# Stick-breaking with two heads of one feature tile a step and softplus in two rounded parts, and GLA products that alternate between the row halves

## The chip, the cores and the metric

The kernel runs on one core of one Trainium2 chip. The metric is the time of one execution on the device in microseconds, the median over several runs. Before the change it is 2219.93 us (three runs, 2217.63 to 2221.23).

## The reference

One layer of a decoder trunk over 1024 tokens of width 1024, in f32. Four causal token mixers work side by side on one wide projection `h @ w_in`: dilated window attention, a convolution module, gated linear attention (GLA) and stick-breaking attention. Each has its own output projection, is gated by a sigmoid of gate logits (also from `w_in`), and the sum goes through `w_out`; a squared-ReLU MLP follows. Two mixers matter here.

Stick-breaking, four heads of 64 features, for a query t and keys s < t:

```
z        = q.k / 8
log_keep = log_sigmoid(-z) where s < t, else 0
after    = sum of log_keep over the keys between s and t
w        = exp(log_sigmoid(z) + after) where s < t, else 0
o        = sum over s of w * v
```

Since log_sigmoid(-z) = -softplus(z) and log_sigmoid(z) = z - softplus(z), w is the exponential of z less a sum of softplus over the keys from s up to t.

GLA, four heads (64 key features, 128 value features), with a gate per token and key feature, in chunks (128 tokens in the kernel): inside a chunk a score of t and s is the sum over features of q k exp(cum_t - cum_s); across chunks a state (64 x 128 a head) is decayed and updated, and each chunk's output is values weighted by the scores plus the queries times the state.

## The kernel before

The stages follow each other in one program: front (adaLN, normalization, convolution), `stage_stick`, `stage_gla`, window attention, merge, tail. Each stage writes out every engine's queue by hand, in a block of its own, and the engines meet only at semaphores; an engine works its queue strictly in that order.

Through the mixers runs a second line of work, the dense projection by `w_in` (`class Dense`). A weight tile of 1024 x 128 is loaded (L125), ScalarE rounds it to fp32r as high part (L131), GpSimd subtracts to get the low part (L137), and `split_product` (L656) multiplies with three fp32r matmuls of 512 columns for each of eight feature tiles. Half of the tokens is one unit of 24 matmuls. In the mixers a unit is cut into three pieces of 9, 9 and 6 matmuls (`pieces`, L170), which TensorE's queue holds between the mixers' own products. `serve` (L183), `lower` (L192) and `move` (L200) do the same work for ScalarE, GpSimd and the DMA queue on SP.

**`stage_stick`** (from L2029). A step n is `STEPS[n] = (Q, r, a)`: a half Q of the queries (512), a key block a of 128 keys, counted downwards, and r, one half of the 128 rows of a feature tile. The two heads of a step are those in half r of the two feature tiles j. There are 24 steps: four segments (Q, r), of 4 and of 8 steps. In a block on the diagonal only the columns from the block on are worked on, so the widths are 128, 256, 384 and 512 columns a head, and the triangle in the block itself is cut by GpSimd (`keep_before`). The work of a step:

- `scores` (L2114): z for both heads, contraction over 64 rows, into `ps_z`.
- VectorE `take_scores` (L2182) scales it to `zs`. ScalarE `logs` (L2228, L2230, L2232): absolute value, Exp, Ln with 1 added. VectorE `softplus` (L2191): max(z, 0) plus that, into `sp_t`.
- `sums` (L2128): `ps_c` gets the product with the triangular matrix `reach`. VectorE `argument` (L2199): zs less `ps_c`. Then `pass_on` (L2138) adds the product with `below`, so that `ps_c` holds the whole block's sum for the next block.
- ScalarE `weights` (L2237) takes the exponential, `values` (L2150) adds w times v to `ps_o`, and `take` (L2204) copies a finished segment.

TensorE's loop is: scores(n), a piece, pass_on(n-2), sums(n-1), a piece, values(n-3). VectorE's is: argument(n-2), softplus(n-1), take_scores(n). ScalarE's is: logs(n), weights(n-2), its share of the dense work. GpSimd's is its dense work, the cut of the softplus of n, the cut of the weights of n-1.

**`stage_gla`** (from L1631) has four blocks. In the second one, the levels, a group is a pair of chunks: 8 matmuls of 128 columns over 64 rows (L1836), four of each row half, into a ring of three results; there are four groups in each of eight levels, and VectorE copies each under a mask (L1878) and prepares the next level's operands (L1866, L1867). A piece follows three of the four groups. The third block is the state loop over eight chunks: `update` (L1909), a piece in the first six, then for each head one product with the scores (L1926) and one with the state (L1929).

An f32 matmul in the source is two instructions in the trace, each with its own weight load; an fp32r matmul is one.

Of the kernel before, what the change touches and what calls it, by code (L numbers as in the profile page):

```python
# [668 lines left out]
def stage_merge(nc, k, dense, w_br):  # L669
# [7 lines left out]
    with ExitStack() as ctx:  # L677
# [21 lines left out]
        def _(sp):  # L699
            def load_y(t):  # L700
# [6 lines left out]
                if t == Y_D:  # L707
                    sp.wait_ge(k.stick_stored, 32)
# [922 lines left out]
def stage_gla(nc, k, w_gate, dense):  # L1631
# [7 lines left out]
    with ExitStack() as outer:  # L1639
# [10 lines left out]
        with ExitStack() as ctx:  # L1650
# [15 lines left out]
            def _(sp):  # L1666
                sp.wait_ge(k.stick_stored, 32)
# [8 lines left out]
            @block.gpsimd  # L1676
            def _(pool):
                pool.wait_ge(k.stick_stored, 32)
                nc.gpsimd.memset(carry[:, :, :, :].rearrange("p c n t -> p (c n t)"), 1.0).then_inc(carry_ready, 1)
                dense.lower(pool, FROM + PREPARE)  # L1680
# [86 lines left out]
        with ExitStack() as ctx:  # L1767
# [51 lines left out]
            def _(pe):  # L1819
                for j in range(LEVELS + 1):  # L1820
                    if j >= 1:
                        pe.wait_ge(parts_ready, 2 * j)
                    for m in range(N_CH // 2):
# [3 lines left out]
                        for r in range(2):  # L1827
                            rows = slice(E * r, E * r + E)
                            for a in range(2):
                                for c in range(2):  # L1830
                                    tok = slice((2 * m + a) * CH, (2 * m + a + 1) * CH)
# [5 lines left out]
                            last.then_inc(scored, 1)  # L1837
# [4 lines left out]
            def _(dve):  # L1842
# [15 lines left out]
                def level_parts(j):  # L1858
                    dve.wait_ge(decayed, j)
                    if j >= 3:  # L1860
                        dve.wait_ge(scored, (j - 1) * N_CH)
# [8 lines left out]
                for j in range(LEVELS + 1):  # L1870
                    if 1 <= j < LEVELS:
                        level_parts(j + 1)
                    for m in range(N_CH // 2):
                        n = j * (N_CH // 2) + m
                        dve.wait_ge(scored, 2 * n + 2)
# [6 lines left out]
        with ExitStack() as late:  # L1882
# [3 lines left out]
            with ExitStack() as ctx:  # L1886
# [16 lines left out]
                def _(pe):  # L1903
# [10 lines left out]
                    for n in range(N_CH):  # L1914
# [114 lines left out]
def stage_stick(nc, k, dense):  # L2029

    FROM = dense.served
    HEAD, EACH = 6, 2
    with ExitStack() as ctx:
        STEPS = [(Q, r, a) for Q in range(NH) for r in range(2) for a in reversed(range(4 * Q + 4))]
        N = len(STEPS)
        HALVES = (HEAD + EACH * (N + 3)) // 3
        qk = ctx.enter_context(nc.sbuf_tensor("sb_qk", [P, 4, S], F32))
        v_tok = ctx.enter_context(nc.sbuf_tensor("sb_v_tok", [P, S // P, SB_HEADS * E], F32))
        below = ctx.enter_context(nc.sbuf_tensor("sb_below", [P, P], F32))
        vT = ctx.enter_context(nc.sbuf_tensor("sb_vT", [P, 2, S], F32))  # L2040
        mag = ctx.enter_context(nc.sbuf_tensor("sb_mag", [P, 2, 2, HALF], F32))
        sp_t = ctx.enter_context(nc.sbuf_tensor("sb_softplus", [P, 2, 2, HALF], F32))
        w = ctx.enter_context(nc.sbuf_tensor("sb_weight", [P, 3, 2, HALF], F32))
        zs = ctx.enter_context(nc.sbuf_tensor("sb_z", [P, 3, 2, HALF], F32))
# [4 lines left out]
        v_loaded, q_loaded, turned, v_copied, below_set = sems(nc, ctx, "sb_v_loaded", "sb_q_loaded", "sb_turned", "sb_v_copied", "sb_below_set")  # L2049
        (z_done, mag_ready, exped, logged, plus_ready, cut, passed, cum_done, arg_ready, w_ready, w_cut, o_done, o_copied,  # L2050
         z_read) = sems(
            nc, ctx, "sb_z_done", "sb_mag_ready", "sb_exped", "sb_logged", "sb_plus_ready", "sb_cut", "sb_passed", "sb_cum_done",
            "sb_arg_ready", "sb_w_ready", "sb_w_cut", "sb_o_done", "sb_o_copied", "sb_z_read")
        block = ctx.enter_context(nc.Block())

        def cols(n):

            Q, r, a = STEPS[n]
            return slice(max(0, a * P - Q * HALF), HALF)

        def diagonal(n):
            Q, r, a = STEPS[n]
            return a >= 4 * Q

        def opens(n):
            Q, r, a = STEPS[n]
# [5 lines left out]
        def segment(n):  # L2072
            Q, r, a = STEPS[n]
            return 2 * Q + r
# [11 lines left out]
        def _(sp):  # L2086
# [6 lines left out]
            heads = k.mix[Y_D * P:Y_TILES * P, :].rearrange("(j r e) s -> j e r s", r=2, e=E)  # L2093
            for j in range(2):
                sp.dma_start(heads[j], yT[E * j:E * j + E, :, :]).then_inc(k.stick_stored, 16)

        @block.tensor
        def _(pe):
# [7 lines left out]
            def scores(n):  # L2106
                Q, r, a = STEPS[n]
# [5 lines left out]
                for j in range(2):  # L2113
                    last = nc.tensor.matmul(ps_z[:, j, c], qk[E * r:E * r + E, 2 + j, a * P:(a + 1) * P],  # L2114
                                            qk[E * r:E * r + E, j, Q * HALF + c.start:(Q + 1) * HALF], start=True, stop=True)
                last.then_inc(z_done, 1)

            def sums(n):
                c = cols(n)
# [3 lines left out]
                if n == 0:  # L2123
                    pe.wait_ge(v_copied, 4)
                if opens(n) and n >= 1:
                    pe.wait_ge(arg_ready, n)
                for j in range(2):
                    last = nc.tensor.matmul(ps_c[:, j, c], k.reach[:, :], sp_t[:, n % 2, j, c], start=opens(n), stop=True, skip_group_check=True)  # L2128
                last.then_inc(cum_done, 1)

            def pass_on(n):
# [3 lines left out]
                c = cols(n)  # L2135
# [199 lines left out]
```

## Time and profile before

| | |
|---|---|
| median of three runs | 2219.93 us |
| profiled execution | 2223.6 us, span 2221.9 us |
| TensorE (PE) busy | 2108.0 us, 95% of the span |
| VectorE (DVE) busy | 943.6 us, 42% |
| ScalarE (ACT) busy | 651.3 us, 29% |
| GpSimd (POOL) busy | 542.2 us, 24% |
| mean granted TensorE clock | 0.978 of full speed |

Times in the trace count from the start of the span. The stick-breaking steps lie at about 525 to 737, GLA's levels at 804 to 915, GLA's state loop at 915 to 957. A matmul's duration includes its way through the array, and the next one starts before it has ended; what a matmul occupies is told by the distance from its start to the next start (its slot).

### The profile page before, as it was taken

The page shows a single profiled execution, that of the slowest core. Times are in us where ns is not written, and L with a number is a line of the kernel's source. Part 1 is how long each engine was busy: PE and PEld are TensorE (multiplying, and loading weights), DVE is VectorE, ACT ScalarE, POOL GpSimd, SP SyncE. Part 2 cuts the span into 40 slices and gives each one's busy share as a digit, 9 for nine tenths or more (in the row PEclk, how much of TensorE's full clock was granted, in tenths as well). Part 3 has the DMA queues.
Part 4 walks back from the last instruction along what each step waited for, and adds up shares of the span by engine and source line. Part 5 has one row for each costly group of instructions (what it writes and reads, how often), then busy time and mean ns, then how long its engine had stood idle before and what let it go on. Part 6 is the DMA issues. An engine that isn't in the chain of part 4 may idle for free. (4 is left out here: it accounts for less than half of the span.)

```text
span 2221.9 us, 23815 instructions
## 1 busy us (share of the span) xinstructions
PE 2108.0 (95%) x9584; PEld 1664.3 (75%) x9584; DVE 943.6 (42%) x1109; ACT 651.3 (29%) x913; POOL 542.2 (24%) x260
## 2 busy tenths in 40 slices
PE   6999999999999989988998799699999999999999
PEld 5878888787655668765787678478888888888887
DVE  6455753012333366333543368453343333334324
ACT  5311111233445222154653233232221221122111
POOL 0112222211211133014201011301343343333332
PEclk9999999999999989999999899899999999999999
DMA  8345553333111411235114476600111111111112
GB/s 276 100 139 167 151 152 95 91 106 122 38 42 39 153 57 39 77 106 193 37 59 142 145 239 218 255 20 20 48 48 48 48 48 57 48 39 52 53 48 95
DMA packets 200550, 216.99 MB, mean 98 GB/s; under 512 B 8778, under 2 KB 156362, under 8 KB 200442
## 3 DMA queue, kind: packets, MB, share of 16 engines
q1 hardware_dynamic: 200272, 215.40, 30.3%
q8 instruction: 77, 1.26, 0.2%
q14 instruction: 31, 0.25, 0.0%
q10 hardware_dynamic: 170, 0.07, 0.0%
HBM read 162.85 MB, written 52.59 MB: 97 GB/s over the span
## 5 line engine op out<-in xcount | busy, mean ns | idle before, releaser
L661 PE MATMUL dn_ps<-h_hi,dn_hi 128*128 128x512 f32 (+1 forms) x1120 | 470.5, 420 | 18.8 <-PEq L60 8.2
L663 PE MATMUL dn_ps<-h_hi,dn_lo 128*128 128x512 f32 (+1 forms) x1120 | 443.3, 396 | 0.0
L662 PE MATMUL dn_ps<-h_lo,dn_hi 128*128 128x512 f32 (+1 forms) x1120 | 442.9, 395 | 0.0
L139 POOL TENSOR_TENSOR dn_lo<-dn_raw,dn_hi 128x1024 fp32r<-128x1024 f32 (+1 forms) x69 | 166.0, 2406 | 691.2 <-ACT dn_hi L135 571.9
L661 PEld LDWEIGHTS dn_ps<-h_hi,dn_hi 128*128 128x128 f32 (+1 forms) x1120 | 213.0, 190 | 92.5 <-issue 41.6
L662 PEld LDWEIGHTS dn_ps<-h_lo,dn_hi 128*128 128x128 f32 (+1 forms) x1120 | 213.3, 190 | 49.5 <-issue 7.2
L663 PEld LDWEIGHTS dn_ps<-h_hi,dn_lo 128*128 128x128 f32 (+1 forms) x1120 | 212.5, 190 | 49.2
L1200 DVE TENSOR_TENSOR tl_x<-tl_x,tl_bank 128x512 f32<-128x512 f32 x256 | 173.2, 686 | 133.1 <-PE tl_bank L663 133.1
L156 ACT ACTIVATE dn_out<-dn_ps 128x512 f32<-128x512 f32 (+1 forms) x138 | 81.9, 593 | 476.3 <-PE dn_ps L663 469.9
L1036 POOL TENSOR_TENSOR tl_w_lo<-tl_raw,tl_w_hi 128x1024 fp32r<-128x1024 f32 x64 | 153.4, 2397 | 231.1 <-ACT tl_w_hi L957 231.1
L661 PE MATMUL tl_bank<-tl_h_hi,tl_w_hi 128*128 128x512 f32 x512 | 199.5, 390 | 0.0
L662 PE MATMUL tl_bank<-tl_h_lo,tl_w_hi 128*128 128x512 f32 x512 | 199.2, 389 | 0.0
L663 PE MATMUL tl_bank<-tl_h_hi,tl_w_lo 128*128 128x512 f32 x512 | 199.2, 389 | 0.0
L661 PE MATMUL tl_bank<-tl_w_hi,tl_u_hi 128*128 128x512 f32 x512 | 199.2, 389 | 0.0
L662 PE MATMUL tl_bank<-tl_w_lo,tl_u_hi 128*128 128x512 f32 x512 | 199.2, 389 | 0.0
L663 PE MATMUL tl_bank<-tl_w_hi,tl_u_lo 128*128 128x512 f32 x512 | 199.2, 389 | 0.0
L1042 POOL TENSOR_TENSOR tl_u_lo<-tl_square,tl_u_hi 128x1024 fp32r<-128x1024 f32 x32 | 104.3, 3259 | 277.5 <-DVE tl_square L1190 277.5
L1190 DVE TENSOR_TENSOR tl_square<-tl_relu 128x1024 f32<-128x1024 f32 x32 | 39.6, 1239 | 306.5 <-ACT tl_relu L988 306.5
L957 ACT ACTIVATE tl_w_hi<-tl_raw 128x1024 fp32r<-128x1024 f32 x64 | 67.8, 1061 | 286.2 <-PE tl_bank L663 226.6
L663 PEld LDWEIGHTS tl_bank<-tl_h_hi,tl_w_lo 128*128 128x128 f32 x512 | 96.1, 188 | 20.0
L661 PEld LDWEIGHTS tl_bank<-tl_h_hi,tl_w_hi 128*128 128x128 f32 x512 | 96.1, 188 | 20.0
L661 PEld LDWEIGHTS tl_bank<-tl_w_hi,tl_u_hi 128*128 128x128 f32 x512 | 96.1, 188 | 19.9
(281 smaller groups left out, 2969.3 us busy)
## 6 DMA issues: line engine op xcount, KB each, us to landing
dn_raw<-w_in_dram SPq DMA_DIRECT2D x70, 512.0 KB, 4.3
ada<-w_ada_dram SPq DMA_DIRECT2D x24, 1024.0 KB, 7.3
proj<-dn_out SPq DMA_DIRECT2D x72, 256.0 KB, 2.2
logits<-dn_out SPq DMA_DIRECT2D x64, 256.0 KB, 2.1
mg_gate<-logits SPq DMA_DIRECT2D x32, 512.0 KB, 5.1
tl_raw<-w_up_dram SPq DMA_DIRECT2D x32, 512.0 KB, 3.9
tl_raw<-w_down_dram SPq DMA_DIRECT2D x32, 512.0 KB, 3.5
wa_qk<-proj SPq DMA_DIRECT2D x6, 1024.0 KB, 16.5
```

The source lines that it names most:

```text
L139: self.nc.gpsimd.tensor_tensor(self.lo_at(j), self.raw_at(j), self.hi_at(j).bitcast(F32), ALU.subtract).then_inc(self.lo_ready, 1)
L156: self.nc.scalar.activation(self.out[0:width, h, :], self.ps[0:width, h, :], ACT.Copy).then_inc(self.copied, 1)
L661: nc.tensor.matmul(out, w_hi[:, t, :], x_hi[:, t, :], start=begin, stop=False)
L662: nc.tensor.matmul(out, w_hi[:, t, :], x_lo[:, t, :], start=False, stop=False)
L663: mm = nc.tensor.matmul(out, w_lo[:, t, :], x_hi[:, t, :], start=False, stop=end)
L957: nc.scalar.activation(dst, raw[:, ring(j)], ACT.Copy).then_inc(hi_ready, 1)
L1036: nc.gpsimd.tensor_tensor(lo, raw[:, ring(j)], hi.bitcast(F32), ALU.subtract).then_inc(lo_ready, 1)
L1042: nc.gpsimd.tensor_tensor(u_lo[:, b % 2, f, :], square[:, n % 2], u_hi[:, b % 2, f, :].bitcast(F32), ALU.subtract).then_inc(u_lo_ready, 1)
L1190: nc.vector.tensor_tensor(square[:, n % 2], relu[:, n % 2], relu[:, n % 2], ALU.mult).then_inc(square_ready, 1)
L1200: nc.vector.tensor_tensor(x1[:, tt, cols], x1[:, tt, cols], bank[:, 4 + n % 4, :], ALU.add).then_inc(summed, 1)
```

## The change

In `stage_stick` a step is now (Q, j, a): the two heads of one feature tile, which lie in its two row halves, in place of the same half of two tiles. The softplus is split: ScalarE copies it to fp32r (`high_softplus`), VectorE subtracts that from it (`low_softplus`, fp32r as well), and `sums` and `pass_on` multiply both parts by fp32r copies of `reach` and `below`. The orders on the engines change with it. In `stage_gla` the loops over the row half move inwards in the levels, and in the state loop the four products with the state follow the four with the scores.

```diff
-        STEPS = [(Q, r, a) for Q in range(NH) for r in range(2) for a in reversed(range(4 * Q + 4))]
+        STEPS = [(Q, j, a) for Q in range(NH) for j in range(2) for a in reversed(range(4 * Q + 4))]
+    LAG = 4
-        HALVES = (HEAD + EACH * (N + 3)) // 3
+        HALVES = (HEAD + EACH * (N + LAG - 1)) // 3
...
-            heads = k.mix[Y_D * P:Y_TILES * P, :].rearrange("(j r e) s -> j e r s", r=2, e=E)
-            for j in range(2):
-                sp.dma_start(heads[j], yT[E * j:E * j + E, :, :]).then_inc(k.stick_stored, 16)
+            sp.dma_start(feature_tiles(k.mix[Y_D * P:Y_TILES * P, :]), yT[:, :, :]).then_inc(k.stick_stored, 16)
...
-                for j in range(2):
-                    last = nc.tensor.matmul(ps_z[:, j, c], qk[E * r:E * r + E, 2 + j, a * P:(a + 1) * P],
+                for r in range(2):
+                    last = nc.tensor.matmul(ps_z[:, r, c], qk[E * r:E * r + E, 2 + j, a * P:(a + 1) * P],
                                             qk[E * r:E * r + E, j, Q * HALF + c.start:(Q + 1) * HALF], start=True, stop=True)
...
+            def add_sums(n, matrix, first):
+                c = cols(n)
+                for r in range(2):
+                    nc.tensor.matmul(ps_c[:, r, c], matrices[:, matrix, :], plus_hi[:, n % 3, r, c], start=first, stop=False, skip_group_check=True)
+                    last = nc.tensor.matmul(ps_c[:, r, c], matrices[:, matrix, :], plus_lo[:, n % 3, r, c], start=False, stop=True, skip_group_check=True)
+                return last
...
             def sums(n):
-                pe.wait_ge(plus_ready, n + 1)
-                if diagonal(n):
-                    pe.wait_ge(cut, 1 + cuts[n + 1])
+                pe.wait_ge(lo_ready, n + 1)
...
-                for j in range(2):
-                    last = nc.tensor.matmul(ps_c[:, j, c], k.reach[:, :], sp_t[:, n % 2, j, c], start=opens(n), stop=True, skip_group_check=True)
-                last.then_inc(cum_done, 1)
+                add_sums(n, 0, opens(n)).then_inc(cum_done, 1)
 
             def pass_on(n):
...
                 pe.wait_ge(arg_ready, n + 1)
-                for j in range(2):
-                    last = nc.tensor.matmul(ps_c[:, j, c], below[:, :], sp_t[:, n % 2, j, c], start=False, stop=True, skip_group_check=True)
-                last.then_inc(passed, 1)
+                add_sums(n, 1, False).then_inc(passed, 1)
...
-            for n in range(N + 3):
+            for n in range(N + LAG):
                 if n < N:
                     scores(n)
-                if n < N + 2:
+                if n < N + LAG - 1:
                     dense.pieces(pe, 1)
+                if 3 <= n < N + 3:
+                    pass_on(n - 3)
                 if 2 <= n < N + 2:
-                    pass_on(n - 2)
-                if 1 <= n <= N:
-                    sums(n - 1)
-                if n < N + 2:
+                    sums(n - 2)
+                if n < N + LAG - 1:
                     dense.pieces(pe, 1)
-                if n >= 3:
-                    values(n - 3)
-            dense.pieces(pe, 3 * HALVES - HEAD - 2 * (N + 2))
+                if n >= LAG:
+                    values(n - LAG)
+            dense.pieces(pe, 3 * HALVES - HEAD - EACH * (N + LAG - 1))
 
         @block.vector
...
+            def low_softplus(n):
+                c = cols(n)
+                dve.wait_ge(hi_ready, n + 1)
+                nc.vector.tensor_tensor(plus_lo[:, n % 3, :, c], plus[:, n % 2, :, c], plus_hi[:, n % 3, :, c].bitcast(F32), ALU.subtract).then_inc(lo_ready, 1)
...
-            for n in range(N + 2):
-                if n >= 2:
-                    argument(n - 2)
+            for n in range(N + 3):
+                if n < N:
+                    take_scores(n)
                 if 1 <= n <= N:
                     softplus(n - 1)
-                if n < N:
-                    take_scores(n)
+                if n >= 3:
+                    argument(n - 3)
+                if 1 <= n <= N:
+                    low_softplus(n - 1)
...
         @block.scalar
...
+            def high_softplus(n):
+                c = cols(n)
+                act.wait_ge(plus_ready, n + 1)
+                if diagonal(n):
+                    act.wait_ge(cut, cuts[n + 1])
+                if n >= 3:
+                    act.wait_ge(cum_done, n - 2)
+                    act.wait_ge(passed, passes[n - 2])
+                nc.scalar.activation(plus_hi[:, n % 3, :, c], plus[:, n % 2, :, c], ACT.Copy).then_inc(hi_ready, 1)
...
-            for n in range(N + 2):
+            for n in range(N + 3):
+                if 1 <= n <= N:
+                    high_softplus(n - 1)
                 if n < N:
                     logs(n)
-                if n >= 2:
-                    weights(n - 2)
+                if n >= 3:
+                    weights(n - 3)
                 dense.serve(act, FROM + halves_before(n))
```

`zs` has a ring of four in place of three, and GpSimd cuts the weights of n-3 before the softplus of n. In GLA:

```diff
-                        for r in range(2):
-                            rows = slice(E * r, E * r + E)
-                            for a in range(2):
-                                for c in range(2):
-                                    tok = slice((2 * m + a) * CH, (2 * m + a + 1) * CH)
+                        for a in range(2):
+                            tok = slice((2 * m + a) * CH, (2 * m + a + 1) * CH)
+                            for c in range(2):
+                                for r in range(2):
+                                    rows = slice(E * r, E * r + E)
...
+                        for h in range(GLA_HEADS):
+                            c, r = h // 2, h % 2
+                            last = nc.tensor.matmul(ps_o[:, n % 2, r, c * P:(c + 1) * P], v_tok[:, n, h * P:(h + 1) * P],
+                                                    att[:, n // 2, r, (2 * (n % 2) + c) * P:(2 * (n % 2) + c + 1) * P],
+                                                    start=(c == 0), stop=(n == 0), skip_group_check=True)
                         if n >= 1:
                             pe.wait_ge(state_ready, 2 * n)
-                        for h in range(GLA_HEADS):
-                            c, r = h // 2, h % 2
-                            dst = ps_o[:, n % 2, r, c * P:(c + 1) * P]
-                            last = nc.tensor.matmul(dst, v_tok[:, n, h * P:(h + 1) * P],
-                                                    att[:, n // 2, r, (2 * (n % 2) + c) * P:(2 * (n % 2) + c + 1) * P], start=True, stop=(n == 0))
-                            if n >= 1:
-                                last = nc.tensor.matmul(dst, state[E * r:E * r + E, n % 2, c, :], q_in[E * r:E * r + E, c, n * CH:(n + 1) * CH],
-                                                        start=False, stop=True)
+                            for h in range(GLA_HEADS):
+                                c, r = h // 2, h % 2
+                                last = nc.tensor.matmul(ps_o[:, n % 2, r, c * P:(c + 1) * P], state[E * r:E * r + E, n % 2, c, :],
+                                                        q_in[E * r:E * r + E, c, n * CH:(n + 1) * CH], start=False, stop=True, skip_group_check=True)
```

## Rows read from the trace of the kernel before

**Rows 1.** The page, busy time (us, share of the span, instructions) of each engine.

```profile
PE 2108.0 (95%) x9584; PEld 1664.3 (75%) x9584; DVE 943.6 (42%) x1109; ACT 651.3 (29%) x913; POOL 542.2 (24%) x260
```

**Rows 2.** Stretches: length, busy us of each engine, PEclk, DMA share, GB/s.

```profile
525.00:737.00 212.00, 211.84 (x790) 128.00 (x789) 72.85 (x79) 96.00 (x123) 37.49 (x41) 1.00 0.15 45
828.00:914.00 86.00, 85.85 (x616) 70.09 (x613) 53.35 (x41) 18.02 (x17) 22.79 (x12) 0.99 0.14 42
915.00:957.00 42.00, 40.41 (x226) 30.17 (x227) 4.31 (x15) 7.61 (x12) 3.30 (x2) 0.98 0.22 76
```

**Rows 3.** Timeline of a wide stick step: start, us, engine, line, operation.

```profile
691.48 1.98 PE L2114 MATMUL sb_ps_z<-sb_qk 64*128 64x512 f32 x4
693.39 0.50 PE L661 MATMUL dn_ps<-h_hi,dn_hi 128*128 128x512 f32 x1
693.50 1.22 DVE L2182 TENSOR_SCALAR sb_z<-sb_ps_z 128x1024 f32<-128x1024 f32 x1 [1.52 <-PE sb_ps_z L2114]
...
695.33 0.39 PE L663 MATMUL dn_ps<-h_hi,dn_lo 128*128 128x512 f32 x1
695.56 1.88 PE L2138 MATMUL sb_ps_c<-sb_softplus,sb_below 128*128 128x512 f32 x4
...
697.28 1.88 PE L2128 MATMUL sb_ps_c<-sb_softplus,reach 128*128 128x512 f32 x4
...
699.19 1.22 DVE L2199 TENSOR_TENSOR sb_weight<-sb_z,sb_ps_c 128x1024 f32<-128x1024 f32 x1 [4.47 <-PE sb_ps_c L2128]
...
700.33 1.22 DVE L2191 SCALAR_TENSOR_TENSOR sb_softplus<-sb_z,sb_mag 128x1024 f32<-128x1024 f32 x1
```

**Rows 4.** The same timeline, the values of a wide step.

```profile
710.94 1.08 PE L2150 MATMUL sb_ps_o<-sb_weight,sb_v_tok 128*64 128x512 f32 x4
711.95 1.55 PE L2114 MATMUL sb_ps_z<-sb_qk 64*128 64x512 f32 x3
```

**Rows 5.** Timeline in the window stage, scores that alternate between the row halves.

```profile
1082.90 1.13 PE L1448 MATMUL wa_ps_s<-wa_qk 64*128 64x256 f32 x8
...
1083.96 0.33 PE L1459 MATMUL wa_ps_t<-ident,wa_prob 128*128 128x128 f32 x1
```

**Rows 6.** Groups by line and shape, 525 to 740: busy us, mean ns, idle before.

```profile
L139 POOL TENSOR_TENSOR dn_lo<-dn_raw,dn_hi 128x1024 fp32r<-128x1024 f32 x9 | 23.2, 2574 | 39.9 <-ACT dn_hi L135 39.9
L2228 ACT ACTIVATE sb_mag<-sb_z 128x1024 f32<-128x1024 f32 x12 | 12.7, 1059 | 57.0 <-DVE sb_z L2182 57.0
L2255 POOL TENSOR_SCALAR_AFFINE_SELECT sb_softplus<-sb_softplus 128x256 f32<-128x256 f32 x16 | 6.5, 406 | 39.7 <-DVE sb_softplus L2191 39.7
L2182 DVE TENSOR_SCALAR sb_z<-sb_ps_z 128x256 f32<-128x256 f32 x4 | 1.7, 422 | 3.3 <-PE sb_ps_z L2114 3.3
```

**Rows 7.** The softplus tile's instructions on VectorE: ns shortest/median/longest, starts, shapes.

```profile
L2191 DVE SCALAR_TENSOR_TENSOR sb_softplus<-sb_z,sb_mag x24: 418/1110/3166, 528.1 to 720.8; 128x1024 f32<-128x1024 f32 x12, 128x256 f32<-128x256 f32 x4, 128x512 f32<-128x512 f32 x4, 128x768 f32<-128x768 f32 x4
```

**Rows 8.** Timeline in GLA's levels: the first wait, and one group.

```profile
825.16 2.45 PE L1836 MATMUL gl_ps_att<-gl_q,gl_k 64*128 64x128 f32 x13 [8.50 <-DVE gl_att L1878]
...
848.13 1.71 PE L1836 MATMUL gl_ps_att<-gl_parts 64*128 64x128 f32 x16
849.77 0.50 PE L661 MATMUL dn_ps<-h_hi,dn_hi 128*128 128x512 f32 x1
```

**Rows 9.** Timeline in GLA's state loop: the first chunk, and the second.

```profile
918.27 1.05 PE L1926 MATMUL gl_ps_o<-gl_att,gl_v_tok 128*128 128x128 f32 x8
919.25 0.66 PE L1909 MATMUL gl_ps_u<-gl_v_tok,gl_k_tok 128*64 128x128 f32 x8
...
922.02 0.38 PE L1926 MATMUL gl_ps_o<-gl_att,gl_v_tok 128*128 128x128 f32 x2
...
925.25 0.66 PE L1909 MATMUL gl_ps_u<-gl_v_tok,gl_k_tok 128*64 128x128 f32 x8
```

**Rows 10.** Stretches, columns as in Rows 2.

```profile
744.00:748.00 4.00, 4.00 (x12) 3.12 (x11) 0.00 (x0) 0.00 (x0) 0.39 (x1) 0.58 0.71 177
975.00:985.00 10.00, 8.00 (x27) 4.99 (x28) 6.81 (x6) 9.84 (x11) 2.81 (x1) 1.00 0.31 116
```

More of the change, by code:

```diff
@@ L1836, in _ @@
                                     last = nc.tensor.matmul(ps[:, n % 3, r, (2 * a + c) * P:(2 * a + c + 1) * P], keys, queries, start=True, stop=True)
-                            last.then_inc(scored, 1)
+                        last.then_inc(scored, 1)
                         if m < 3:
@@ L2072, in segment @@
         def segment(n):
-            Q, r, a = STEPS[n]
-            return 2 * Q + r
+            Q, j, a = STEPS[n]
+            return 2 * Q + j
         cuts, passes = [0], [0]
@@ L2106, in scores @@
             def scores(n):
-                Q, r, a = STEPS[n]
+                Q, j, a = STEPS[n]
                 if n == 0:
@@ L2148, in values @@
                     pe.wait_ge(o_copied, segment(n) - 1)
-                for j in range(2):
-                    last = nc.tensor.matmul(ps_o[E * j:E * j + E, segment(n) % 2, c], v_tok[:, a, (2 * j + r) * E:(2 * j + r + 1) * E],
-                                            w[:, n % 3, j, c], start=opens(n), stop=closes(n), skip_group_check=True)
+                for r in range(2):
+                    last = nc.tensor.matmul(ps_o[E * r:E * r + E, segment(n) % 2, c], v_tok[:, a, (2 * j + r) * E:(2 * j + r + 1) * E],
+                                            w[:, n % 3, r, c], start=opens(n), stop=closes(n), skip_group_check=True)
                 last.then_inc(o_done, 1)
@@ L2209, in _ @@
                 nc.vector.tensor_copy(v_tok[:, 2 * i:2 * i + 2, :].rearrange("p u e -> p (u e)"), bank).then_inc(v_copied, 1)
-            for n in range(N + 2):
-                if n >= 2:
-                    argument(n - 2)
+            for n in range(N + 3):
+                if n < N:
+                    take_scores(n)
                 if 1 <= n <= N:
                     softplus(n - 1)
-                if n < N:
-                    take_scores(n)
-                if n >= 4 and closes(n - 4):
-                    take(segment(n - 4))
-            take(3)
+                if n >= 3:
+                    argument(n - 3)
+                if 1 <= n <= N:
+                    low_softplus(n - 1)
+                if n >= LAG + 1 and closes(n - LAG - 1):
+                    take(segment(n - LAG - 1))
+            for n in range(N + 3, N + LAG + 1):
+                if closes(n - LAG - 1):
+                    take(segment(n - LAG - 1))
         @block.scalar
@@ L2239, in _ @@
             nc.scalar.preload_act_table_set("natural_log_exp_and_others")
+            nc.scalar.activation(matrices[:, 0, :], k.reach[:, :], ACT.Copy).then_inc(matrices_ready, 1)
+            act.wait_ge(below_cut, 1)
+            nc.scalar.activation(matrices[:, 1, :], below[:, :], ACT.Copy).then_inc(matrices_ready, 1)
             dense.serve(act, FROM + 1)
-            for n in range(N + 2):
+            for n in range(N + 3):
+                if 1 <= n <= N:
+                    high_softplus(n - 1)
                 if n < N:
                     logs(n)
-                if n >= 2:
-                    weights(n - 2)
+                if n >= 3:
+                    weights(n - 3)
                 dense.serve(act, FROM + halves_before(n))
@@ L2250, in _, with keep_before @@
         def _(pool):
-            def keep_before(tile, ring, n):
-                c = cols(n)
-                own = tile[:, n % ring, :, c.start:c.start + P]
+            def keep_before(own):
                 return nc.gpsimd.affine_select(out=own, in_=own, compare_op=ALU.is_gt, fill=0.0, base=0,
@@ L2261, in _ @@
             nc.gpsimd.affine_select(out=below[:, :], in_=below[:, :], compare_op=ALU.is_gt, fill=0.0,
-                                    base=0, pattern=[[1, P]], channel_multiplier=-1).then_inc(cut, 1)
-            for n in range(N + 1):
+                                    base=0, pattern=[[1, P]], channel_multiplier=-1).then_inc(below_cut, 1)
+            for n in range(N + 3):
                 dense.lower(pool, FROM + min(HALVES, halves_before(n - 1) + 1) if n else FROM + 1)
+                if n >= 3 and diagonal(n - 3):
+                    at = cols(n - 3).start
+                    pool.wait_ge(w_ready, n - 2)
+                    keep_before(w[:, (n - 3) % 3, :, at:at + P]).then_inc(w_cut, 1)
                 if n < N and diagonal(n):
+                    at = cols(n).start
                     pool.wait_ge(plus_ready, n + 1)
-                    keep_before(sp_t, 2, n).then_inc(cut, 1)
-                if n >= 1 and diagonal(n - 1):
-                    pool.wait_ge(w_ready, n)
-                    keep_before(w, 3, n - 1).then_inc(w_cut, 1)
+                    keep_before(plus[:, n % 2, :, at:at + P]).then_inc(cut, 1)
             dense.lower(pool, FROM + HALVES)
```

59 lines of the change are left out of this document (31 added, 28 removed).

## The prediction

> **What bounds the kernel now.** I read the page first, then the busy time by stage, then the timeline of one step in each stage that the change touches. TensorE is busy for 95% of the span [rows 1]. In the three stretches at issue it is busy nearly throughout: the stick-breaking steps (525 to 737), GLA's levels (828 to 914) and GLA's state loop (915 to 957), while no other engine passes 62% [rows 2]. The stages follow each other on one TensorE queue, so a microsecond taken from that queue there is a microsecond of the span, as long as nothing else comes to end the waits.
>
> A full-width stick step in TensorE's slots (start to next start): scores 1.91 (691.48 to 693.39), a dense product of 0.23 (695.33 to 695.56), `below` 1.72 (695.56 to 697.28), values 1.01 (710.94 to 711.95) [rows 3, 4]. `reach` has the same four 512-column passes as `below`: 1.72. A piece is 6 or 9 products, 8 on average: 1.84. Sum: 1.91 + 2 x 1.72 + 1.01 + 2 x 1.84 = 10.0 us.
>
> **Part 1, stick-breaking on TensorE.** There are 24 steps, 12 of 512 columns and four each of 384, 256 and 128; `below` is left out in four wide ones. I scale the slots with the width.
> - `reach` and `below`: each head had one f32 matmul, two passes of 0.43; now it has two fp32r matmuls, which I price as the dense ones, 0.23. A wide pair of heads falls from 1.72 to 0.92. No row shows fp32r below 512 columns. From below, 0.23 x width/512; from above, at 128 columns, twice the f32 pass, which is 0.43 / 4 = 0.107 there. I take 0.11 at 128 columns, where f32 already stands, and above it about the proportional value. The high bound costs 32 matmuls x 0.1 = 3 us. Total: 31.0 + 24.2 before, 17.5 + 13.8 after.
> - Scores: both heads used the same row half, so four passes ran one after another. Now the halves alternate. The window stage already does this: eight 256-column passes, 1.70 if serial, took 1.06 (1082.90 to 1083.96), that is four pairs of 0.213 and 0.21 over [rows 5]. Four 512-column passes become 2 x 0.43 + 0.21 = 1.07, for 1.91; total 34.8 to 20.3. Values alternate output halves before and after: 19.2 either way.
> - Pieces: 54 of them before and after (two used to stand behind the loop), 99.4.
>
> TensorE's work falls from 208.6 to 170.3. The first sum checks: the stretch lasted 212 and two pieces followed, less 1 us of edges 214.8. The missing 6.2 is 0.2 a step for changes of shape.
>
> **But the new order makes VectorE's chain count.** Before, VectorE's first work in a step was the argument, whose sums lay a piece and a set of values back, so `below` found it done. Now VectorE does take_scores(n), softplus(n-1), argument(n-3), and TensorE's queue holds scores(n), one piece, then `below`(n-3), which waits for that argument. take_scores cannot start before scores(n) is done: at 0.11 after the slot (693.50 for 693.39) [rows 3]. Three wide operations of 1.22 at a pitch of 1.14 (699.19 to 700.33) [rows 3] need 3.50; with that 0.11, 0.05 for the semaphore and 0.09 for the first weight load, 3.75, against a piece of 1.84. TensorE waits 1.9 us in every wide step, with `below`, the sums, the second piece and the values all queued behind. A wide step is 1.07 + 3.75 + 0.92 + 0.92 + 1.84 + 1.01 = 9.5, not the 7.6 of its work. With the narrow operation at 0.42 [rows 6] and widths between in proportion, the chain of passes 3 to 23 adds up to 62.6 where their first pieces are 38.6. The loop: scores 20.3, values 19.2, sums 17.5, `below` 13.8, 27 second pieces 49.7, six first pieces uncovered by a chain (passes 0 to 2 and 24 to 26) 11.0, chain 62.6: 194.1. I add 0.15 a pass for changes of shape, 4.2.
>
> ScalarE gets one more operation a step, 1.06 wide [rows 6], some 20 us in all on the 96.0 of [rows 2]: 116 in 200. Within a wide step its order is high half, three logs, weights, dense copies: about 6.1 of 9.5, so the logarithm is there when VectorE comes for it, and I cost it at nothing; at a step of 6.1 the cover would be gone. VectorE's low part (about 1.2) lies behind the argument, while TensorE works on; it waits for the high half, and on diagonal steps for GpSimd's cut of 0.41 [rows 6], still inside the 5.7 before the next scores. GpSimd's own queue has the nine dense low parts of 2.57 [rows 6]. They start when ScalarE has made a dense high part, at the end of its step, which now falls onto the softplus of the next one. One softplus before took 3.17 where 1.22 is usual [rows 3, 7]; I read that as the two engines being in each other's way. That was hidden; now it is in the chain. Bounds: nothing, or 9 x 1.95 = 18. I take 4, since half are in narrow steps or miss it. Stick stage: 194.1 + 4.2 + 4 = 202.3, for 214.8: **12.5 us gained**.
>
> The store of the result is one DMA for two and waits for the same last copy; the two matrices are rounded while TensorE does its six head pieces. Both at nothing (0.5 at most either way).
>
> **Part 2, GLA's levels.** A group of 16 passes of 128 columns, eight with each half, takes 1.64 (848.13 to 849.77) [rows 8]: serial would be 1.71. Interleaved it is eight pairs of 0.107 and the 0.21 over of [rows 5]: 1.07, a gain of 0.57. Of 32 groups the first three gain nothing, because TensorE then waits 8.5 us for VectorE before the fourth, at 825.16 [rows 8]. 29 x 0.57 = **16.5 us**. VectorE has the room: in 828 to 914 it was busy 53 of 86 us [rows 2], and 86 - 16.5 leaves 69.5. Its order there (both parts of the next level, then four copies) keeps three result buffers apart from TensorE's next group.
>
> The Trainium skill ("TensorE: Matmul & The Clock Gate", "Part 3: Packing small matmuls — row/col tiling") gives packed tiles a span of one matmul and some 4 ns for each further tile. By that rule a group would be near 0.87 and this term about 22 us; my row of the window stage shows more over, so the sum goes by the row.
>
> **Part 3, the state loop.** Products with the levels' weights (all 128 rows) and with the state (64 rows) alternated in twos: 3.23 from 922.02 to 925.25 [rows 9]. Now eight full passes come first, 0.98 as in the first chunk (918.27 to 919.25) [rows 9], then eight state passes as four pairs, 0.43 + 0.21 = 0.64. Gain 3.23 - 1.62 = 1.61 in seven chunks: **11.3 us**. The wait for the state now stands later, and it was met before.
>
> **Sum.** 12.5 + 16.5 + 11.3 = 40.3, with 0.5 for the store 41 us. The profiled execution took 2223.6 (span 2221.9), 3.7 above the median of 2219.93. 2223.6 - 41 = 2182.6; against the median, 2179.
>
> **Rivals.**
> - *TensorE stays the bound in the stick steps*, if VectorE runs ahead of my chain. For it: the work is 170.3 + 6. Against it: take_scores cannot precede the scores. Gain 38 instead of 12.5: 2153; halfway, with the packing of the rule above, 2160. Chance 0.15.
> - *VectorE's chain grows*: each of the nine dense low parts costs its 1.95, and narrow fp32r the high price. Loss 14 + 3 against my sum: 2196. If the alternating scores bring only half their 14.5 as well, 2203. Chance 0.2.
> - *The order of the halves brings nothing* since the array already overlaps what it can (1.64 is below 1.71). Then parts 2 and half of 3 go, and the scores: 2179 + 16.5 + 4 + 14.5 = 2214. The window's row speaks against it. Chance 0.04.
> - *Slower: the clock falls in the stick steps.* Gaps of 1.9 come back in every wide step, where TensorE had none. At 744 to 748, after an idle stretch, the granted clock was 0.58, near the lower level of 1.2 GHz [rows 10]. Time at the half clock loses half of itself, so 82 of the stage's 202 us at that level eat the 41, and the whole stage there gives 2179 + 101 = 2280; with half the stage, 2229. Against it: at 975 to 985 TensorE was busy 80% with waits for ScalarE and kept 1.00 [rows 10], and these steps are at 80% too. Chance 0.06. [...]
>
> **Numbers.** Forecast 2179, chance 0.55, with 2170 to 2188 as its own range. With the rivals the range for eight in ten is 2158 to 2202. A difference of 0.2%, some 4 us, is about what a measurement tells from none. Faster by more than that: 0.55 + 0.15 + 0.2 + 0.03 = 0.93; within it 0.02; slower 0.05.
>
> **What would show it.** In the stick steps: scores 1.07, fp32r passes at 0.23, and before `below` an idle TensorE of 1.9 in wide steps, released by VectorE's argument; a stage of 202. If that idle time is missing, the first rival holds. Level groups at 1.07 and an end of the levels 16 us nearer to their start; a chunk's products at 1.6. The granted clock stays near 1.00. I am wrong if the level groups stay at 1.64, or if the softplus is long in most steps.

## The result

| | before | changed kernel |
|---|---|---|
| median | 2220.01 us (4 runs, 2217.63 to 2221.23) | 2180.73 us (4 runs, 2178.50 to 2185.93) |
| ratio | | 0.983, 95% interval 0.981 to 0.984 |
| profiled execution, span | 2223.6, 2221.9 | 2178.5, 2176.4 |

The change takes 39.3 us between the medians; 41 were forecast, 2179 for 2180.73. The two profiled executions stand further apart, 45.5 in the span (the one before lies 3.6 above its median, the changed one 2.2 below), and I use them to place the gain, not to size it. Distances between first instructions of each part, on TensorE, subtracted before rounding:

| stretch | before | changed | less |
|---|---|---|---|
| start to the first stick scores | 525.3 | 525.0 | 0.3 |
| stick steps, their store, to GLA's gate product (L1688) | 225.2 | 209.3 | 15.8 |
| GLA's preparation, to the levels | 53.5 | 52.0 | 1.6 |
| levels, to the state loop | 111.5 | 97.9 | 13.6 |
| state loop, to the first product of the norm | 47.8 | 33.8 | 14.0 |
| the rest | 1258.6 | 1258.4 | 0.2 |

The 1.6 of GLA's preparation is the clock: in its first 10 us the granted clock was 0.87 and 0.79 before (750.5 to 760.5, by halves) and 1.00 in the changed kernel. It comes and goes whatever the kernel: the traces of the experiments below have 51.9 to 55.2 there.

### The profile page after: what moved, and what is told of

The parts are those of the page before. It is cut to its first block and busy times, and to the rows that moved or that the text cites. A ratio compares the mean times of both kernels' runs of the same rounds, so it can differ in the third digit from the quotient of the medians.

```text
span 2176.4 us, 23882 instructions
## 1 busy us (share of the span) xinstructions
PE 2040.8 (94%) x9584; PEld 1625.4 (75%) x9584; DVE 975.4 (45%) x1133; ACT 669.0 (31%) x939; POOL 541.8 (25%) x260
## 5 line engine op out<-in xcount | busy, mean ns | idle before, releaser
L661 PE MATMUL dn_ps<-h_hi,dn_hi 128*128 128x512 f32 (+1 forms) x1120 | 460.8, 411 | 20.2 <-PEq L60 8.3
```

The source lines that it names most:

```text
L661: nc.tensor.matmul(out, w_hi[:, t, :], x_hi[:, t, :], start=begin, stop=False)
```

## The profile after

The stick stage, the levels and the state loop in the changed kernel, with the columns of [rows 2]; the last row is a part of the stick stage:

```profile
525.00:727.00 202.00, 181.60 (x800) 118.54 (x800) 100.85 (x101) 115.25 (x149) 36.70 (x41) 0.99 0.16 48
809.00:882.00 73.00, 73.00 (x616) 57.28 (x616) 55.51 (x41) 16.65 (x17) 24.21 (x12) 0.98 0.16 48
884.00:914.00 30.00, 28.69 (x225) 23.62 (x226) 4.13 (x14) 7.11 (x12) 2.79 (x2) 1.00 0.31 106
690.00:695.00 5.00, 2.83 (x7) 2.26 (x8) 3.33 (x3) 3.92 (x4) 0.00 (x0) 0.68 0.04 11
```

Before, TensorE was busy for all of the stick stage [rows 2]; now 20 of 202 us are idle. TensorE's waits between 525 and 735 say for what (us in total, times, longest; the last one is at the end of the stage):

```profile
PE sb_ps_c L2125 <- DVE sb_weight L2208: 18.1, 15, 3.0
PE dn_ps L661 <- ACT dn_out L156: 2.2, 3, 1.0
PE dn_ps L661 <- PEq L2035: 1.7, 1, 1.7
```

L2125 is the high product of the sums, L2208 the argument: the wait that the prediction put there. The timeline of a wide step shows the chain, to be read against [rows 3]:

```profile
698.49 1.13 PE L2118 MATMUL sb_ps_z<-sb_qk 64*128 64x512 f32 x4
699.55 0.50 PE L661 MATMUL dn_ps<-h_hi,dn_hi 128*128 128x512 f32 x1
699.67 1.23 DVE L2186 TENSOR_SCALAR sb_z<-sb_ps_z 128x1024 f32<-128x1024 f32 x1 [6.34 <-PE sb_ps_z L2118]
...
700.81 1.21 DVE L2195 SCALAR_TENSOR_TENSOR sb_softplus<-sb_z,sb_mag 128x1024 f32<-128x1024 f32 x1
...
701.94 1.21 DVE L2208 TENSOR_TENSOR sb_weight<-sb_z,sb_ps_c 128x1024 f32<-128x1024 f32 x1
...
703.21 0.50 PE L2125 MATMUL sb_ps_c<-sb_plus_hi,sb_matrices 128*128 128x512 f32 x1 [1.32 <-DVE sb_weight L2208]
703.54 0.40 PE L2126 MATMUL sb_ps_c<-sb_plus_lo,sb_matrices 128*128 128x512 f32 x1
703.78 0.40 PE L2125 MATMUL sb_ps_c<-sb_plus_hi,sb_matrices 128*128 128x512 f32 x1
```

Scores occupy 1.06 (698.49 to 699.55; 1.91 before), an fp32r product 0.23, and from the end of the scores' slot to `below` pass 3.66 us, against 3.75 in the prediction, with this step's piece of nine products, 2.07, to fill them. A piece has nine or six products, so the wait is 1.32 here and 2.0 behind a piece of six (in e5 below); the prediction's 1.9 took the mean of eight. One step earlier a dense low part of GpSimd lies on the softplus:

```profile
687.52 2.38 POOL L139 TENSOR_TENSOR dn_lo<-dn_raw,dn_hi 128x1024 fp32r<-128x1024 f32 x1 [1.03 <-ACT dn_hi L135]
687.61 1.22 DVE L2186 TENSOR_SCALAR sb_z<-sb_ps_z 128x1024 f32<-128x1024 f32 x1 [4.20 <-PE sb_ps_z L2118]
...
688.75 2.23 DVE L2195 SCALAR_TENSOR_TENSOR sb_softplus<-sb_z,sb_mag 128x1024 f32<-128x1024 f32 x1
...
692.16 0.79 PE L2125 MATMUL sb_ps_c<-sb_plus_hi,sb_matrices 128*128 128x512 f32 x1 [3.02 <-DVE sb_weight L2208]
...
692.76 0.63 PE L2126 MATMUL sb_ps_c<-sb_plus_lo,sb_matrices 128*128 128x512 f32 x1
```

The softplus starts at 688.75 and ends at 690.98, 1.08 after GpSimd is done (689.90): nearly its whole usual time lies behind GpSimd's instruction. TensorE waits 3.02, and the matmuls that follow take 0.63 with 0.43 from start to start, where 0.40 and 0.23 are usual: the half clock, 0.68 granted on average in 690 to 695. Of the 24 softplus instructions this happened to two (2.23 here and 2.95 at 638.28). The other one made TensorE wait as long, and the clock stayed:

```profile
642.41 0.50 PE L2125 MATMUL sb_ps_c<-sb_plus_hi,sb_matrices 128*128 128x512 f32 x1 [2.94 <-DVE sb_weight L2208]
642.75 0.40 PE L2126 MATMUL sb_ps_c<-sb_plus_lo,sb_matrices 128*128 128x512 f32 x1
```

`take_scores`, at the same time as the same GpSimd instruction, kept its 1.22. It reads one input, from PSUM; softplus and the low part read two from SBUF, and the low part took 2.10 to 2.27 in the steps of this trace where GpSimd had started before it. In the kernel before, a wide softplus started first, at 700.33, and kept its 1.22 [rows 3]; there GpSimd's instruction was the long one, 3.31 for some 2.37:

```profile
700.45 3.31 POOL L139 TENSOR_TENSOR dn_lo<-dn_raw,dn_hi 128x1024 fp32r<-128x1024 f32 x1 [1.04 <-ACT dn_hi L135]
```

The Trainium skill ("VectorE: DVE Perf Modes", "Two Vector instructions with no wait between them") says by the way that an operation with two SBUF inputs reads the second through an interface shared with GpSimd; the trace agrees with that.

A group of GLA's levels, then two groups back to back, which answer to [rows 8]:

```profile
847.79 1.16 PE L1836 MATMUL gl_ps_att<-gl_parts 64*128 64x128 f32 x16
848.88 0.50 PE L661 MATMUL dn_ps<-h_hi,dn_hi 128*128 128x512 f32 x1
...
850.47 2.06 PE L1836 MATMUL gl_ps_att<-gl_parts 64*128 64x128 f32 x32
852.46 0.50 PE L661 MATMUL dn_ps<-h_hi,dn_hi 128*128 128x512 f32 x1
```

And two groups back to back in the kernel before:

```profile
851.36 2.82 PE L1836 MATMUL gl_ps_att<-gl_parts 64*128 64x128 f32 x32
...
854.10 0.19 PEld L661 LDWEIGHTS dn_ps<-h_hi,dn_hi 128*128 128x128 f32 x1
```

A single group fell from 1.64 to 1.09, but the pair at each change of level from 2.74 to 1.99, by 0.75 and not by twice 0.55. A chunk of the state loop, against [rows 9]:

```profile
898.83 1.05 PE L1923 MATMUL gl_ps_o<-gl_att,gl_v_tok 128*128 128x128 f32 x8
899.81 0.71 PE L1930 MATMUL gl_ps_o<-gl_q_decayed,gl_state 64*128 64x128 f32 x8
900.45 0.66 PE L1909 MATMUL gl_ps_u<-gl_v_tok,gl_k_tok 128*64 128x128 f32 x8
```

0.98 and 0.64: 1.62, for 3.23, as predicted; seven times that is 11.3 of the 14.0 us. The other 2.7 us are the clock. The start of the norm's dense pieces, before and then changed:

```profile
956.00:964.00 8.00, 7.75 (x20) 5.92 (x21) 0.00 (x0) 4.12 (x4) 2.38 (x1) 0.60 0.01 2
```

```profile
917.00:925.00 8.00, 8.00 (x29) 5.03 (x28) 2.83 (x3) 5.80 (x6) 0.00 (x0) 1.00 0.01 2
```

## The experiments

**The two parts apart.** e1 is the changed kernel with GLA as before, e2 the kernel before with the changed GLA.

```diff
 e1: def stage_gla(...)     as before, waiting for 16 in place of 32 on stick_stored
 e2: def stage_gla(...)     as changed, waiting for 32; stage_stick as before
```

> Stick-breaking as after the change, GLA as before. My theory (the two parts add, each on TensorE's queue): the loop from the first scores to the last values takes 202 us, the store lands some 2 us sooner, so 13 to 16 us less than before, near 2205; the state loop still ends in a stretch at the half clock. Rival (the 39 us are mostly one part, and the stick steps, with their new waits, give little): within 5 us of before.

> GLA as after the change, stick-breaking as before. My theory: levels 14 us less (the two groups that stand back to back at each change of level overlapped already), state loop 11 us less, and 0 to 3 us more if the half-clock stretch behind the state loop goes: 25 to 28 us less, near 2193. Rival (the clock, not the order of the halves, gave much of it): under 20 us less.

e1: 2206.77 us, ratio 0.994 (0.992 to 0.995), 13.4 less than before (2220.21 in these rounds). e2: 2193.23, ratio 0.988 (0.986 to 0.989), 27.0 less. The sum, 40.4, is the 39.3 of the whole change within the scatter: the parts add. One part of e1's expectation failed: behind its state loop the clock stayed at 1.00 (942 to 948), and a half-clock stretch stood at the loop's start (0.86 granted in 903 to 913). In e2's trace the levels take 98.7 and the stretch from the state loop to the norm 33.7; in e1, with the old GLA, they take 112.0 and 46.2. With the old loop that stretch varied, 47.8, 46.2 and 46.3 in three traces; with the new one it was 33.7 to 33.8 in all of six. e4, the third trace with the old loop, had its half clock behind the loop again (0.73 in 940 to 943, 0.70 in 943 to 946). The chunks are worth 11.3 by their slots, and the 12.5 against e1 and e4 hold this clock as well.

**VectorE's order put back.** e3 is the changed kernel but for this:

```diff
             for n in range(N + 3):
-                if n < N:
-                    take_scores(n)
+                if n >= 3:
+                    argument(n - 3)
                 if 1 <= n <= N:
                     softplus(n - 1)
-                if n >= 3:
-                    argument(n - 3)
+                if n < N:
+                    take_scores(n)
                 if 1 <= n <= N:
                     low_softplus(n - 1)
```

> The changed kernel with VectorE's order put back to argument, softplus, take_scores, then the low part. My theory (the chain scores, take_scores, softplus, argument holds `below` up): TensorE's 18 us of waits for the argument go, and what a long softplus added, 17 to 22 us less than the changed kernel, near 2161. Rival (ScalarE is next: with its five wide operations and the dense copies it is late with the logarithm or the high half once the step is shorter): the waits only move there, under 8 us less. Slower if take_scores, now third, makes ScalarE late in each step.

2151.15 us, ratio to before 0.968 (0.967 to 0.970), 29.6 less than the changed kernel. The wait for the argument is gone, and TensorE has no idle time in the loop (525 to 700, columns as above):

```profile
525.00:700.00 175.00, 174.93 (x800) 118.94 (x800) 96.19 (x102) 116.94 (x149) 40.57 (x41) 1.00 0.19 56
```

From the first scores to the start of the last pass of values it took 174.4 (524.9 to 699.3), for 201.4 in the changed kernel (525.0 to 726.4). My theory stands in kind, and was too low in size: 27 us went from the loop, not 17 to 22. The 18.1 of recorded waits starts only when the last matmul has left the array, 0.17 after its slot has ended, so 15 waits cost another 2.5; each has a first weight load behind it, another 1.5; the piece's wait for a copy (2.2) went as well; and the half clock was some 1.5. That is 26 of the 27. The two traces stand 30.1 apart, 27.0 of it in the loop and 2.9 behind the first product of the norm, where the kernels are the same and which I take for scatter. ScalarE, the rival, was busy 117 of 175 and not late. No softplus took more than 1.23 there: the same GpSimd instructions now lay on `take_scores` and on the low part, so the 27 us hold the contention too.

**Only the pairing of the heads.** e4 is the kernel before, in its old order and with f32 sums, but the two heads of one feature tile to a step.

```diff
-                for j in range(2):
-                    last = nc.tensor.matmul(ps_z[:, j, c], qk[E * r:E * r + E, 2 + j, a * P:(a + 1) * P],
+                for r in range(2):
+                    last = nc.tensor.matmul(ps_z[:, r, c], qk[E * r:E * r + E, 2 + j, a * P:(a + 1) * P],
```

> Before, with only the pairing of the heads changed (scores alternate between the row halves, f32 sums, old order, the store still two DMAs of 64 rows). My theory: the four wide score passes take 1.07 in place of 1.91 us, 14.5 us less over 24 steps, since TensorE is the bound in the old order: near 2205. Rival (alternating halves only helps short passes): 5 us less or none.

2205.01 us, ratio 0.993 (0.991 to 0.995), 15.2 less; in the traces the loop, from the first scores to the start of the last pass of values, fell from 210.5 to 194.8. So passes of 512 columns overlap as well as the short ones, and the pairing by itself, in the old order, brings as much as the whole stick part of the change (13.4, e1).

**The sums by themselves.** e6 is the changed kernel with f32 sums.

```diff
-                    nc.tensor.matmul(ps_c[:, r, c], matrices[:, matrix, :], plus_hi[:, n % 3, r, c], start=first, stop=False, ...)
-                    last = nc.tensor.matmul(ps_c[:, r, c], matrices[:, matrix, :], plus_lo[:, n % 3, r, c], start=False, stop=True, ...)
+                    last = nc.tensor.matmul(ps_c[:, r, c], (below if matrix else k.reach)[:, :], plus_lo[:, n % 3, r, c], start=first, stop=True, ...)
```

> The changed kernel with the sums as one f32 matmul a head again. The two operations that split softplus stay, the second one now takes the larger of the value and its rounded copy and writes f32, so orders and waits are the same. My theory (sums and `below` stand in TensorE's queue behind the wait, so nothing hides them): 31.0 + 24.2 for 17.5 + 13.8, 24 us more than the changed kernel, near 2204. Rival (the waits for the argument swallow part of it): under 12 us more.

2204.93 us, 24.2 more than the changed kernel; wide sums are back at a slot above 1.8:

```profile
708.92 1.98 PE L2125 MATMUL sb_ps_c<-sb_plus_lo,sb_below 128*128 128x512 f32 x4 [2.00 <-DVE sb_weight L2207]
710.75 1.88 PE L2125 MATMUL sb_ps_c<-sb_plus_lo,reach 128*128 128x512 f32 x4
```

The wait for the argument stays beside them (18.1 us in all, as in the changed kernel), as it must if the sums lie behind it; only the pieces' wait for a copy fell, from 2.2 to 0.8. The loop took 224.2 in the traces (523.8 to 748.1), 22.9 more than the changed kernel's. The 24.2 compares medians taken apart: against the kernel before of their own rounds the two kernels stand 21.6 apart. So the time alone can't tell the low price of narrow fp32r products from the high bound, 3 us dearer. Their slots can, in the trace of the changed kernel:

```profile
614.45 0.34 PE L2126 MATMUL sb_ps_c<-sb_plus_lo,sb_matrices 128*128 128x384 f32 x1
614.63 0.34 PE L2125 MATMUL sb_ps_c<-sb_plus_hi,sb_matrices 128*128 128x384 f32 x1
...
658.91 0.27 PE L2125 MATMUL sb_ps_c<-sb_plus_hi,sb_matrices 128*128 128x128 f32 x1
659.02 0.28 PE L2126 MATMUL sb_ps_c<-sb_plus_lo,sb_matrices 128*128 128x128 f32 x1
```

0.18 and 0.11 from start to start; at 256 columns it is 0.12. That is the low price as forecast: 0.11 at 128 columns, where f32 stands too, and proportional above.

**GpSimd's dense low parts out of softplus's way.** e5 is the changed kernel with one wait:

```diff
             for n in range(N + 3):
+                if 1 <= n <= N:
+                    pool.wait_ge(lo_ready, n)
                 dense.lower(pool, FROM + min(HALVES, halves_before(n - 1) + 1) if n else FROM + 1)
```

> The changed kernel with one wait more: GpSimd starts a dense low part only when VectorE's low part of that step is done, when VectorE has nothing to do until the next scores. My theory (the dense low parts stretch softplus, which is now in the chain): every wide softplus is back at 1.22, TensorE's longest wait for the argument falls from 3.0 to about 1.9, the half-clock stretches behind the long waits go too, 4 to 8 us less than the changed kernel. Rival (the long softplus has another cause, or the dense low parts now come late for TensorE's pieces): no difference, or slower.

2173.38 us (five rounds, 2172.73 to 2178.03, ratio 0.979, 0.978 to 0.980), 7.4 below the changed kernel's median, and 9.9 if each is set against the kernel before of its own rounds. Softplus in the changed kernel (shortest/median/longest ns), then the wide softplus by shape in e5 (busy us, mean ns, idle before), then TensorE's wait for the argument in e5:

```profile
L2195 DVE SCALAR_TENSOR_TENSOR sb_softplus<-sb_z,sb_mag x24: 415/1081/2948, 531.1 to 706.3; 128x1024 f32<-128x1024 f32 x12, 128x256 f32<-128x256 f32 x4, 128x512 f32<-128x512 f32 x4, 128x768 f32<-128x768 f32 x4
```

```profile
L2195 DVE SCALAR_TENSOR_TENSOR sb_softplus<-sb_z,sb_mag 128x1024 f32<-128x1024 f32 x12 | 14.6, 1216 | 1.9 <-ACT sb_mag L2245 1.9
```

```profile
PE sb_ps_c L2125 <- DVE sb_weight L2208: 15.3, 15, 2.0
```

The longest wait fell from 3.0 to 2.0, the total from 18.1 to 15.3. The loop, to the start of the last pass of values, took 197.1 (523.7 to 720.8) for 201.4. These 4.3 are the size that the traces place in the stage: 2.8 of waits and, by estimate from the 0.68 below, some 1.5 of half clock. The rest of the 7.4 lies outside it: 1.3 before the first scores, where the kernels are the same, and between the rounds. Of sixteen stretches of 5 us between 640 and 720 the changed kernel had one at 0.68; e5 had no stretch of the stage under 0.95.

**The store.** e7 is the changed kernel with its result in two DMAs of 64 partitions.

```diff
-            sp.dma_start(feature_tiles(k.mix[Y_D * P:Y_TILES * P, :]), yT[:, :, :]).then_inc(k.stick_stored, 16)
+            for r in range(2):
+                sp.dma_start(heads[r], yT[E * r:E * r + E, :, :]).then_inc(k.stick_stored, 16)
```

> The changed kernel with its result stored by two DMAs of 64 partitions each, as before, in place of one of 128. My theory: from issue to the next load 6.5 in place of 4.3 us, with TensorE waiting behind it, 2 us more. Rival (the shorter time came from an emptier queue): no difference.

2184.77 us, 4.0 above the changed kernel's median, but the kernel before was 2222.59 in those rounds and 2220.01 in the changed kernel's, so some 1.5 to 4 us. The DMA queue shows the landing more sharply. Issue of the store and of the load that waits for it, changed kernel and then e7:

```profile
727.73 0.37 SPq L2099 DMA_DIRECT2D mix<-sb_yT  x1
732.05 0.32 SPq L1669 DMA_DIRECT2D gl_low<-proj  x1
```

```profile
728.38 1.32 SPq L2101 DMA_DIRECT2D mix<-sb_yT  x2
734.91 0.32 SPq L1669 DMA_DIRECT2D gl_low<-proj  x1
```

4.32 us for one, 6.53 for two. All traces with one store show 4.3, all with two (before, e2, e4) 6.5.

My theory has the landing right and the path wrong: TensorE doesn't wait behind that load. Three dense pieces lie between the stick stage and the gate product, and the gate product starts 0.3 us after their last matmul has started, in both traces. What differs is the first matmul of these pieces, changed kernel and then e7:

```profile
728.70 0.47 PE L661 MATMUL dn_ps<-h_hi,dn_hi 128*128 128x512 f32 x1 [1.74 <-PEq L2035]
```

```profile
730.55 0.76 PE L661 MATMUL dn_ps<-h_hi,dn_hi 128*128 128x512 f32 x1 [2.93 <-PEq L2035]
```

L2035 is the `with` line of `stage_stick`: TensorE stands at the end of the stage, so the engines meet there too, and not only at the semaphores that the stages' code names. Its next matmul starts 0.60 to 0.63 us after SP has issued a single store and 0.84 after the second of two, in all nine traces. Two issues take 1.32 us and one 0.37, so TensorE waits 1.2 longer. Then the three pieces take 7.18 for 5.64, with 0.50 granted in 731.5 to 733.5. The five traces with one store have waits of 1.7 to 1.8 and pieces of 5.6 to 5.7; the four with two have 2.9 to 3.2 and 7.2 to 8.4. The load would come next: without the half clock the pieces of e7 would end near 736.2, and the gate's weights, issued at 735.28, take 1.9 to land (an estimate from these two traces).

## Why the prediction was right, point by point

- **Stick stage, 12.5 us forecast.** Forecast for the loop to the end of the last values: 202.3, for 214.8. Measured: 525.0 to 726.4, and 0.4 for the last pass, 201.8, for 214.6 (525.3 to the end of the two pieces behind the loop, 739.9). It is made up as written: scores 1.06 for the 1.07, products 0.23, the chain 3.66 for 3.75. e5, without the contention on softplus, took 197.5 counted in the same way, and the forecast without its 4 us for that was 198.3. e3, without the chain, took 174.8; the work was put at 170.3 and 4.2 for changes of shape, 174.5.
- **The contention, 4 us.** 4.3 in the traces, 7.4 between medians. The size is right with some luck. I had taken about half of nine low parts at up to 1.95 each; two of them met a softplus, for 2.7 us together (2.8 of TensorE's waits), and six others lay on VectorE's low part, which took up to 2.27 there without a wait of TensorE. The rest is the half clock after one of the two long waits, which I had not priced.
- **The store, 0.5 at most.** Mis-sized: the stretch from the end of the last piece or values to the gate product was 10.4 before and is 7.4 now, 3.1 less. Of these 1.45 are idle time at the end of the stage (3.19 and now 1.74), where TensorE waits until SP has issued the store, and 1.6 are the three pieces behind it (7.25 and now 5.64), which before ran in part at the half clock [rows 10]. I had asked only when the store's data is ready and had not looked at what TensorE waits for there. The landing, 2.2 us sooner, is not on its path.
- **Levels, 16.5 us.** 13.6 in the traces (13.3 in e2 against e1). Mis-sized by the groups that stand back to back: two of them took 2.74 for what I took as 3.28, so the array already let matmuls of one run beside matmuls of the next where the halves meet (the trace has two that start within 0.01 us there). Seven such pairs give 0.75 where I had 1.14: 2.7 us.
- **State loop, 11.3 us.** The chunks are as forecast. The stretch gave 14.0 in the profiled pair because that execution before had a half-clock stretch behind the loop, and 12.5 against e1 and e4, whose half-clock stretches were shorter.
- **The rivals.** ScalarE, costed at nothing, was late only with dense copies, 2.2 us in all. The clock fell once in the changed kernel's stage, for some 3 us. Narrow fp32r products had the low price of the forecast. The first rival, TensorE as the bound, was false for this order and is true of e3: 2153 was its time, 2151.15 is e3's.

The mechanism of each part is as forecast, but that the total came within 2 us is partly luck, since the errors cancelled: levels 3 too high, state loop and its clock 1 to 3 too low, the end of the stick stage 2.6 too low. The profiled pair has another 1.6 of clock in GLA's preparation.

What stays open: why a half-clock stretch lay in or behind the old state loop in all three traces, at different places, and in none of six with the new one. TensorE's idle time behind the loop is no answer, since it was 1.1 us in all nine. Nothing here tells whether it was the loop's alternation between 128 and 64 rows.

## What to carry to other kernels

When an order on one engine is changed, follow for every wait which instructions the engine that is waited for does first: here two operations of 1.2 us in front of the argument, which TensorE waits for, cost some 27 us (29.6 between medians) of a gain that the same kernel has with VectorE's order put back (2151.15 us, the fastest version here). Products over 64 rows should alternate between the row halves from one matmul to the next; here the two halves always wrote to different parts of the result tile, and no run shows what happens where they don't. The end of a stage is a wait like any other: ask which engine arrives there last. And what an engine off the critical path was free to stretch before (a softplus under GpSimd's subtraction) must be priced again once it is in the chain.

## What the runs showed of the hardware that I had not expected

- Groups of passes over 64 rows overlap by themselves where one half's run ends and the other's begins, also across groups: 32 passes took 2.74 us, two groups apart 3.28. With the halves in alternation it is 1.99 and 2.18.
- One DMA of 1 MB from 128 partitions let the load behind it go after 4.3 us, two of 0.5 MB from 64 partitions after 6.5.
- An fp32r product of 128 columns occupied 0.11 us, as much as one of the two passes of an f32 product; at 512 columns 0.23 against 0.43.
- A VectorE operation with two SBUF inputs that starts during GpSimd's subtraction ends some 1.1 us after the subtraction is over (2.23, in another step 2.95, for 1.22), as if it had stood still; where it starts first it keeps its 1.22 and GpSimd takes 3.31 for 2.37. One that reads PSUM does not notice (`take_scores` and the argument, 1.22).
- After a wait of 3.02 us TensorE ran at the half clock for about 3 us (0.50 granted in 692 to 695), after one of 2.94 in the same trace it did not. In e5's stick stage, with waits up to 2.0, there was no such stretch; but in the kernel before one lay behind an idle time of only 1.1 us (956 to 964, 0.60). So the length of the last wait doesn't decide it alone.
